# Hybrid encoder layer on one core: a pair's preparation and its end laid out anew beside the attention heads and the pair loop

## The reference, cut to what matters

```python
w_log = -jax.nn.softplus(-(w0 + jnp.tanh(w_l) @ w2)) - 0.5
decay = jnp.exp(-jnp.exp(w_log))
a = jax.nn.sigmoid(a0 + a_l @ a2)
g = jax.nn.sigmoid(g_l) @ g2
kk = heads(k * k_k)
kk = kk / jnp.maximum(jnp.sqrt(jnp.sum(kk * kk, axis=-1, keepdims=True)), 1e-12)
k = k * (1.0 + (a - 1.0) * k_a)
y = wkv7(rh, heads(decay), kh, vh, -kk, kk * ah)      # the recurrence over time
y = (y - mean(y)) * lax.rsqrt(var(y) + GN_EPS) * ln_w + ln_b      # per head of 64
y = y + jnp.sum(rh * kh * r_k, axis=-1, keepdims=True) * vh       # the bonus term
out = y * g
```

## Time and profile before

| | |
|---|---|
| Time, median of 3 runs | 2211.9 us (2209.99 to 2212.21) |
| The profiled execution: its own time, its span | 2225.95 us, 2224.2 us |
| PE busy, share of the span | 2005.1 us, 90% |
| DVE busy | 779.9 us, 35% |
| POOL busy | 493.8 us, 22% |
| ACT busy | 396.1 us, 18% |
| Mean granted PE clock | 0.932 |

### The profile page before, as it was taken

The page is one execution under the profiler, slowest core; times in us unless marked ns, Lnnn a source line. Parts: engine busy times, 40 slices in busy tenths (PEclk is TensorE's granted clock), DMA queues, the critical chain, the costliest instruction groups (busy, mean ns, idle before and its releaser), DMA issues.

```text
span 2224.2 us, 26560 instructions
## 1 busy us (share of the span) xinstructions
PE 2005.1 (90%) x10448; PEld 1591.5 (72%) x10448; DVE 779.9 (35%) x1123; ACT 396.1 (18%) x743; POOL 493.8 (22%) x289
## 2 busy tenths in 40 slices
PE   5999999995789898985988987989999999999996
PEld 4866666654677777763877854867888888888885
DVE  6522323244354555335335035234212212211233
ACT  3122122231212121112003022012101101100110
POOL 2210212011102020002302301223333433333430
PEclk9899899986697989986999999989999999999998
DMA  5000010000111010203123100111111111111111
GB/s 196 29 29 17 19 36 17 3 10 23 46 26 42 24 46 23 61 13 132 47 85 96 53 3 19 38 38 38 47 47 47 47 49 47 55 48 47 47 47 76
DMA packets 76359, 100.90 MB, mean 45 GB/s; under 512 B 28928, under 2 KB 56064, under 8 KB 76032
## 3 DMA queue, kind: packets, MB, share of 16 engines
q1 hardware_dynamic: 76288, 99.90, 14.4%
HBM read 86.76 MB, written 13.12 MB: 45 GB/s over the span
## 4 chain that ended last, share of the span: by engine, by line
PE 83%; DVE 11%; issue 2%; ACT 2%; DMA 1%; POOL 1%; SPq 0%; DVEq 0%; ACTq 0%; POOLq 0%
PE PS L703 44%; PE PS L744 6%; PE PS L873 3%; PE PS L844 3%; PE PS L1291 1%; PE PS L858 1%; PE PS L1075 1%; PE PS L898 1%; DVE tmp L1664 1%; DVE sc_w L1970 1%; PE PS L1228 1%; PE PS L1110 1%; PE PS L1111 1%; PE PS L1085 1%; PE PS L1059 1%
## 5 line engine op out<-in xcount | busy, mean ns | idle before, releaser
L703 PE MATMUL PS<-xn,wsp 128*128 128x512 f32 x2880 | 664.9, 393 | 16.4 <-DVE xn L1657 13.4
L703 PEld LDWEIGHTS PS<-xn,wsp 128*128 128x128 f32 x2880 | 545.3, 190 | 135.2 <-issue 11.6
L703 PE MATMUL PS<-hid,wsp 128*128 128x512 f32 x1536 | 348.8, 389 | 0.0
L703 PEld LDWEIGHTS PS<-hid,wsp 128*128 128x128 f32 x1536 | 288.4, 188 | 59.8
L573 POOL CAST wsp<-wraw 128x1024 fp32r<-128x1024 f32 x104 | 110.4, 1062 | 990.3 <-PE PS L703 695.4
L575 POOL TENSOR_TENSOR wsp<-wraw,wsp 128x1024 fp32r<-128x1024 f32 x104 | 282.8, 2719 | 8.3
L744 PE MATMUL PS<-xn,wsp 128*128 128x512 f32 x576 | 149.9, 407 | 4.2 <-DVE proj L1707 4.2
L744 PEld LDWEIGHTS PS<-xn,wsp 128*128 128x128 f32 x576 | 106.8, 193 | 35.8 <-issue 15.1
L1628 ACT ACTIVATE tmp<-PS 128x1024 f32<-128x1024 f32 x32 | 32.9, 1028 | 494.1 <-PE PS L703 494.1
L2199 DVE TENSOR_TENSOR tmp<-tmp 128x1024 f32<-128x1024 f32 x32 | 39.2, 1225 | 211.7 <-ACT tmp L1628 211.7
L2214 DVE TENSOR_TENSOR H<-PS,H 128x1024 f32 x24 | 29.4, 1224 | 218.6 <-PE PS L703 218.6
(11 more groups left out here) (270 smaller groups left out, 2438.1 us busy)
## 6 DMA issues: line engine op xcount, KB each, us to landing
wraw<-in_weights_dram SPq DMA_DIRECT2D x120, 512.0 KB, 3.5
H<-in_x_dram SPq DMA_DIRECT2D x16, 512.0 KB, 6.8
a_dram<-H SPq DMA_DIRECT2D x16, 256.0 KB, 2.3
H<-x_dram SPq DMA_DIRECT2D x32, 128.0 KB, 2.6
H<-xt_dram SPq DMA_DIRECT2D x32, 128.0 KB, 2.7
out_dram<-proj SPq DMA_DIRECT2D x8, 512.0 KB, 3.0
o_dram<-o_stage SPq DMA_DIRECT2D x3, 512.0 KB, 2.7
ssum<-in_head_weights_dram SPq DMA_DIRECT2D x4, 320.0 KB, 4.1
```

Source lines behind the costliest of these rows:

```text
L703: last = nc.tensor.matmul(PS[:, 2 * k + half, :], wsp[:, k, kt, a, :], src[:, kt, b, HALF * half:HALF * half + HALF], start=(kt == 0 and ( ...
```

## The change

`prep` and `post` get other steps and other places.

- The key's norm and the group norm: instead of `head_sums`, a small DVE step, a POOL power on 16 columns and two `spread`s, two `block_sums` (128x512 matmuls with a matrix of ones per head) leave each sum already spread, and ACT takes `Ln` of each half and `Exp` with scale -1/2 of the whole. DVE then does one multiplication over 1024 columns instead of two over 512. In `post`, gain and bias go into the two remaining DVE steps.
- Places: `prep` now spreads its steps over places 2 to 36, one or two steps on each engine at a place; the 15 inversion steps take places 28 to 35, two to a place. `post` has places 0 to 11 and is called with `s - POST`, `POST = 22`, so a pair's end lies in places 22 to 33 of the next pair.
- Beside heads 6 and 7 every position takes two places (`2*i + 1, 2*i + 2`), so that all of pair 0's preparation lies there. What ended the fourth attention pair becomes `attention_end(s)` in places 1, 5, 6, 7 of pair 0's loop.
- Homes: the bonus terms get four places in memory instead of two; the scan's mask becomes a tile of its own, filled by POOL at the start; `rAL` and the first attention outputs move.
- SP: `inverse` is split into `blocks` and `inverse`; the gate weights move behind the next pair's `inverse`, and each loop turn first reloads one attention output (512 KB).

```diff
-EARLY, SLOTS = 14, 44
-RP_SET = 8
+SLOTS = 44
+POST = 22
+RP_SET = 6
...
-        o_places = [hs_[:, 0:1024], hs_[:, 2048:3072], proj[:, T_K, :], o_stage[:, :]]
+        o_places = [hs_[:, 7168:8192], proj[:, T_K, :], proj[:, T_K + 1, :], o_stage[:, :]]
...
-        rBV = [proj[:, T_CQ, :], proj[:, T_CKV, :]]
+        rStep = step[:, :]
+        rBV = [proj[:, t, :] for t in (T_CQ, T_CKV, T_V, T_V + 1)]
...
         def beside_heads(h, q):
-            s = 9 * (h - BESIDE) + q - 2
-            return s if h >= BESIDE and 0 <= s < EARLY else None
+            i = 9 * (h - BESIDE) + q
+            return (2 * i + 1, 2 * i + 2) if h >= BESIDE else ()
...
             lora_first(0)
+            lora_gate(0)
             store_o(2)
-            sp.wait_ge(M_PE.sem, M_PE.at(f"mt{PAIRS - 1}_1", -1))
-            lora_gate(0)
+            blocks(0)
             inverse(0)
+            sp.wait_ge(o_stored, 16 * (PAIRS - 1))
             for p in range(PAIRS):
                 if p < PAIRS - 1:
+                    sp.dma_start(o_places[p], o_dram[p]).then_inc(o_loaded, 16)
+                if p < PAIRS - 1:
                     lora_first(p + 1)
+                if p < PAIRS - 1:
+                    blocks(p + 1)
+                    inverse(p + 1)
                 if p >= 1:
                     lora_gate(p)
-                if p < PAIRS - 1:
-                    inverse(p + 1)
...
-                if s == 4:
-                    r_at(P_ACT, f"ta1_{n}")
-                    head_sums(rBh[i], 7).then_inc(sem_, one("kks"))
-                if s == 8:
-                    r_at(P_POOL, f"pow_{n}")
-                    r_at(P_DVE, f"kkm_{n}")
-                    spread(pSt, 0, 7).then_inc(sem_, one("kkb0"))
-                if s == 9:
-                    r_at(P_DVE, f"nkk0_{n}")
-                    spread(pSt, 1, 7).then_inc(sem_, one("kkb1"))
+                if s == 6:
+                    r_at(P_ACT, f"kksq_{n}")
+                    block_sums(0, C_BO, rBh[i], 7).then_inc(sem_, one("ks0"))
+                if s == 7:
+                    r_at(P_ACT, f"kl0_{n}")
+                    block_sums(1, C_BO, rBh[i], 7).then_inc(sem_, one("ks1"))
...
+                if s in (6, 7):
+                    r_at(P_PE, f"ks{s - 6}_{n}")
+                    nc.scalar.activation(rB[i][:, halves(s - 6)], PS[:, 7, :], ACT.Ln).then_inc(sem_, one(f"kl{s - 6}"))
+                if s == 7:
+                    r_at(P_ACT, f"kl1_{n}")
+                    nc.scalar.activation(rB[i], rB[i], ACT.Exp, scale=-0.5).then_inc(sem_, one("kf"))
...
             def beside(p, s):
                 if p >= 1:
-                    post(p - 1, s)
+                    post(p - 1, s - POST)
+                else:
+                    attention_end(s)
                 if p < PAIRS - 1:
                     prep(p + 1, s)
...
-            for s in range(EARLY, SLOTS):
-                prep(0, s)
```

More of the change, by code:

```diff
@@ L87, in constants @@
     c[:, C_BM:C_BM + P] = same / HD
-    c[:, C_HO:C_HO + 2] = part // HD == free[:, :2]
+    c[:, C_GE] = GN_EPS
     c[:, C_ONE] = 1.0
@@ L183, in build @@
         small = sb("small", [P, 64])
[L184 removed]
+        rsm = sb("rsm", [HD, 64])
+        step = sb("step", [P, S])
         tmp = sb("tmp", [P, 2, S])
@@ L355, in each @@
             return [f"{x}_{n}" for n in range(PAIRS) for x in names]
-        P_PE = Steps(sem("prep_pe"), each(["lw0", "lw1", "la0", "la1", "kks", "kkb0", "kkb1", "rk0", "rk1",
+        P_PE = Steps(sem("prep_pe"), each(["lw0", "lw1", "la0", "la1", "ks0", "ks1", "rk0", "rk1",
                                            "al0", "al1", "al2", "al3"]))
-        P_ACT = Steps(sem("prep_act"), each(["tw0", "tw1", "kksq", "ta0", "ta1", "W", "Wi", "wt0", "wt1", "afirst"]))
+        P_ACT = Steps(sem("prep_act"), each(["tw0", "tw1", "ta0", "ta1", "kksq", "kl0", "kl1", "kf", "W", "Wi", "wt0", "wt1", "afirst"]))
         P_DVE = Steps(sem("prep_dve"), each(
[L361 to L366, removed]
-        O_POOL = Steps(sem("post_pool"), each(["gpow"]))
+            ["kk", "t1p", "L", "na", "nkk", "am", "k2", "kt", "at", "b", "bt", "rk",
+             "bv0", "bv1", "al0", "al1", "al2", "al3", "x0", "x1"]
+            + [x for j in range(BLK - 1) for x in (f"xm{j}", f"xa{j}")] + ["xt"]))
+        P_POOL = Steps(sem("prep_pool"), each(["rt", "kh", "bh"]))
+        O_PE = Steps(sem("post_pe"), each(["mean0", "mean1", "vs0", "vs1", "lg0", "lg1"]))
+        O_ACT = Steps(sem("post_act"), each(["ysq", "vl0", "vl1", "vf"]))
+        O_DVE = Steps(sem("post_dve"), each(["yc0", "yc1", "yn", "yb", "out0", "out1"]))
         l_pe, l_act, l_dve, l_pool = ["sc0_0", "sc0_1", "tok0_0", "tok0_1", "akv0_0", "akv0_1"], [], ["sc0_0", "sc0_1"], []
@@ L1171, in _, with attention_end @@
             whole(fill)
-            for half in range(2):
-                turn_o(PAIRS - 1, half)
-            for s in range(EARLY, SLOTS):
-                prep(0, s)
+            def attention_end(s):
+                if s in (6, 7):
+                    turn_o(PAIRS - 1, s - 6)
             pe.wait_ge(rp_dve, RP_SET)
```

327 lines of the change are left out of this document (149 added, 178 removed).

## The result

The changed kernel takes 2182.0 us (median of four runs, 2172.9 to 2185.6) against 2212.1 us before: a ratio of 0.985, with a 95% interval of 0.982 to 0.989. The kernel is faster by some 30 us, where 59 were forecast; 2182 us lies 29 us above the forecast and 4 us above the end of the range. One execution of the experiment *e10_one_switch* took 2627 us at a mean granted clock of 0.715 and is left out of its figures. A second profile of each kernel was taken later (runs *before_again*, *after_again*). The profile that the prediction was worked from had a time of 2226 us, 14 above the median; the second one of the same kernel, 2211.8 us, is nearly the median itself.

What follows compares the result with a forecast made beforehand. PE was busy over 90% of heads and loop, with a gap of waiting between them. Gap -37, heads 6 and 7 +8, loop -26, pair 3's end -4 sum to -59: 2211.9 - 59 = 2153 us, range 2136 to 2178.

Steps and rivals of the forecast that it cites:

- The gap: Stretch between last attention head and loop: falls from 52.2 to about 15 us, -37 us (-40 to -32).
- Rival (d): Between heads and loop: block path late, first double_q waits 5 to 8 us; 2160 us; chance 0.06.
- Heads 6 and 7: Last two heads, with pair 0's preparation beside them: +8 us (0 to +18).
- Waits 7.7, work 2.7, less 2.4: Heads 6 and 7: new PE waits plus added PE work, less what idle time takes up, give +8 us.
- rival (a): Heads don't hide the work (+18), loop gives back only PE time (-6): 2183 us; chance 0.17.
- The count of loads and their length: ScalarE: a load per turn to Ln and per turn back, 18 more (27 instead of 9), 1.28 us each.
- rival (c): ScalarE: a table switch drains first, 1.4 us more each, bare five times; 2160 us; chance 0.05.
- The loop: Pairs 0 to 3: -9, -6, -5, -6, together -26 us (-41 to -6).
- The clock: in pair 1 it fell: Loop: clock fell behind head_sums; with these gone, 2.5 us of clock loss stays in each of pairs 1 to 3.
- The end: Pair 3's end, at half clock: about 21.1 us against 25.0, -4 us (-5 to -2).
- (b): Rival, loop: without two-column matmuls the clock stays full, -41 us there; 2138 us; chance 0.20.
- (e): Rival, loop: DVE waits for Exp at place 30 or 10, stopping state-step copies; slower, needing over 63 us; chance 0.02.

Runs made afterwards that it cites:

- e10_one_switch: Changed kernel with both logarithms of end and preparation ahead of both Exp, two table loads instead of four in pairs 1 and 2: 2171.5 us, ratio 0.981.

## Why the prediction was wrong in size

**The sum.** Against the second profile of before, the stages give: heads 0 to 5 -8.8, heads 6 and 7 +17.1, gap -33.3, loop +1.4, pair 3's end -3.8, the rest -0.4; together -27.8, and 2210.0 - 27.8 = 2182.2. The prediction said +8, -37, -26 and -4, so -59 where its four terms measured -18.6. Gap and end came as it had them; the terms of heads and loop failed, both by the clock. That the whole missed by only 29 us owes 9 us to heads 0 to 5, which stood in no term: that is luck.

**The gap: right.** 13 us were said from the last head's end to the first `double_q`, 12.1 came. Windows and low-rank weights were in time: the state tiles, first scores and transposes fill it. -33 us and -37 differ mostly by the stall at place 0 (5.2 us in before), which the landmark puts into pair 0. Rival (d) did not happen.

**Heads 6 and 7: the direct cost right, the step "Waits 7.7, work 2.7, less 2.4" failed by what it left out.** At full clock the two heads take 75.5 us, against 69.2 and 70.1 before: +5.4 to +6.3 where +8 stood. The waits measured 0.8 (`la0`, said 1.0), 1.7 (`ks0`, 1.8), none at `rk0` (2.0), 0.8 and 0.8 (`al0`, `al2`, 0.7 each), and 2.8 behind ScalarE's loads and `Exp` where 1.5 was let through. But the clock fell at them: 20.5 us lost instead of 5.8 and 8.8. No term of the part priced that, though its rows showed PE's waits and a clock of 0.93 together. This is the half of rival (a) that came true; its +18 is what was measured (+17 to +21), with another mechanism than "all waits and all work uncovered". The part also misread a column, which changed little: the 32.7 us given as ScalarE's busy time in the earlier trace rows are DVE's, ScalarE has 27.8, so 2.4 us were free in a position and not 2.2, and 2.7 us would stick out instead of 3.1.

**The count of loads and their length: right, their cost in the loop wrong.** 18 loads more, 1.28 us each. ScalarE's lines of table loads:

```profile
L1403 ACT ACT_TABLE_LOAD x5 | 6.4, 1283 | 0.1
L1406 ACT ACT_TABLE_LOAD x4 | 5.1, 1283 | 0.1
L1436 ACT ACT_TABLE_LOAD x4 | 5.1, 1283 | 0.1
L1440 ACT ACT_TABLE_LOAD x4 | 5.1, 1283 | 0.1
```

and one at L1357. The function follows at once on each load that nothing else holds up (722.85 + 1.28 = 724.13, `Exp` at 724.14): the longer switch of rival (c) isn't there. By the Trainium skill's page ScalarE: Activation LUTs, section Table sets: the hidden batching unit, `Ln` and `Exp` could share one load; in this trace each `Exp` behind a `Ln` has its own. The prediction gave the loop 2 us for queueing; without loads the loop was 12 to 19 us shorter, most of it clock. In the heads, where I had feared them, leaving them out changed little: 97.5 and 92.4 us against 96.0.

**The loop: the length at full clock right, the clock wrong.** 100.3 us were said for pairs 1 and 2 at full clock; 99.9 and 100.6 came. What failed is the step "The clock: in pair 1 it fell [...] right behind `head_sums` [...] These are gone, so I let 2.5 us of clock loss stay". The order of two events in one trace was taken for a cause. The roots alone removed every `head_sums` and left 39.2 us of loss; the matmuls ahead of the state steps removed none of the work and left 8.4. As far as these two runs show, the falls follow TensorE's waits, and the change moved these about and did not end them: the waits of over 0.05 us sum to 10.4, 11.9 and 12.2 us in pairs 0 to 2, against 15.7, 10.8 and 10.9 before, and in pairs 1 to 3 the clock took 5.8 to 16.2 us each instead of 2.5. The differences were also taken from a profile whose loop lost 45.0 us, where another of the same kernel lost 27.3. That is 18 us of the 24 that the forecast meant to win back from the clock, and it had noted itself that the profile was 14 us above the median.

At full clock the loop did get shorter, 383.0 and 385.7 before, 372.8 and 377.9 after, so 5 to 13 us. Of the time really taken, from profile to profile, between 1 us more and 20 us less is left of it.

**The end: right.** 21.5 us against 21.1 said, 25.3 before, and the roots alone give it too.

**Rivals (b) and (e).** A clock that stays full (2138 us) did not come by itself, and the extra matmuls show what a nearly full one is worth: 10 to 16 us in the loop after their own cost. Its -41 us was also added up wrong: -26 less the 17.5 us of clock loss that the forecast let stay gives -43.5. The place that rival (e) named is real, 2.50 us of idle PE at 727.75, a quarter of what it would have needed per end.

**Left open.** Heads 0 to 5 took 307 us in most kernels built on the changed one and 315 to 319 in all four profiles of kernels built on before, with 305 to 306 at full clock in each; that is 9 of the 30 us measured. A part is the change's own, though no term of the prediction had it: at the end of head 5 the kernel before has VectorE fill the scan's mask, and PE waits for it, where the changed kernel waits 0.42 us.

```profile
438.95 2.97 PE L873 MATMUL PS<-tmp,H 128*128 128x64 f32 x16 [1.62 <-DVE H L1800]
```

In all four profiles of kernels built on before low clock begins 0.7 to 2.1 us behind the start of this step (here at 439.7) and costs 1.5 to 2.8 us up to head 6. The rest is not settled. It is stretches of 3.4 and 13.7 us near 258, 266 and 371 us, each 1 to 2 us behind a wait of 1.1 us for VectorE's `o_stage`, and these waits stand in both kernels: the one at 264.62 in before was followed by 13.7 us of low clock, the same at 266.14 in the changed kernel by none, and in three other kernels with its code by 13.7 us again (313.2, 314.8 and 314.8 us). So this part of the gain may not be the change's own. Nor is it settled why the extra matmuls pay in the changed loop and not in the one before, beyond pair 0's stretch from the gap.

## What to carry to other kernels

Price a wait of a TensorE that is nearly full in two parts: its length, and what the granted clock takes behind it. Here 6 us of new waits came with 12 to 15 us more of clock loss, and a few matmuls that nobody needs, put where TensorE waits anyway, gave more back than they cost: the whole fell by 14 us with those in the loop and by 10 with those in the heads, whose own stage shows 5. In the loop of the kernel before the same matmuls gave nothing, so it has to be tried. Take such differences at full clock, stage by stage, and from more than one profile before building on the clock of any. And before a root moves to ScalarE's `Ln` and `Exp`, look which of its functions stand between them: every turn was a load of 1.28 us here, and leaving out those of the preparation shortened the loop by 14 to 20 us.

## What the runs showed that was not expected

- Low clock is far from idle: between 476.3 and 490.0 us PE was busy 13.70 of 13.70 us at a granted clock of 0.50. In the heads of the changed kernel the falls behind waits of 0.8 to 2.8 us last 3.4 to 13.7 us. By the Trainium skill's page TensorE: Matmul & The Clock Gate, section HAM oscillation — how this bites in real kernels, waits for DMAs between short bursts of matmuls bring the clock down again and again, and the loop is to be ordered so that TensorE stays busy. The waits here are short ones for VectorE and ScalarE; as far as the remedy goes the filled loop agrees, 8.4 us lost instead of 30 to 42.
- Not each wait brings a fall: the same 2.50 us of idle PE ahead of the same state step, at 727.75 in pair 1 and at 839.8 in pair 2, was followed by low clock in the first and not in the second. In the second profile of the same kernel both were, at 727.3 and 836.5. One profile's stretches of low clock are a sample.
- The loop of the kernel before lost 45.0 us to the clock in one profile and 27.3 in another, with 383.0 and 385.7 us at full clock: the length at full clock repeats within 1 to 2%, the clock does not.
